# Last head of a fused retention and HGRN2 layer: its keys turned by VectorE and DMA, its level products 4 to 7 in pairs, and one output block's evacuations spread over four weight chunks

## The reference, cut to what matters

```python
h = rms_norm(x, norm_w) * (1 + scale) + shift
rq, rk, rv, rg, hq, hf_f, hf_b, hi, hg = split(h @ w_in, 9)
# retention, forward and on the flipped tokens
o_r = rms_norm(o_rf + flip(o_rb)) * silu(rg)
# HGRN2: f = lb + (1 - lb) * sigmoid(z), k = 1 - f, b = cumsum(log f) in a chunk
scores[i, j] = sum_d q[i, d] * k[j, d] * exp(b[i, d] - b[j, d])      # j <= i
o = scores @ v + (q * exp(b)) @ S
S = exp(b_last) * S + (k * exp(b_last - b)).T @ v
o_h = rms_norm(o_hf + flip(o_hb), hg_norm_w) * silu(hg)
y = rms_norm(x + gate * (concat(o_r, o_h) @ w_out), final_norm_w)
```

## Time and profile before

| | |
|---|---|
| median of 3 runs | 1402.6 us (1402.54 to 1402.9) |
| the profiled execution's own time | 1402.41 us |
| its span, first to last instruction | 1400.6 us |
| granted TensorE clock, mean | 0.999 of full speed |
| TensorE busy | 1383.0 us, 99% |
| VectorE / ScalarE / GpSimd busy | 1000.2 / 483.8 / 368.6 us |
| last head's scans among the first output block | about 1156 to 1227 us of the span |
| TensorE's last product ends | about 1392 us |

### The profile page before, as it was taken

The page is one execution under the profiler, slowest core; times in us unless marked ns, Lnnn a source line. Parts: engine busy times, 40 slices in busy tenths (PEclk is TensorE's granted clock), DMA queues, the critical chain, the costliest instruction groups (busy, mean ns, idle before and its releaser), DMA issues.

```text
span 1400.6 us, 24706 instructions
## 1 busy us (share of the span) xinstructions
PE 1383.0 (99%) x10042; PEld 1165.1 (83%) x10042; DVE 1000.2 (71%) x1330; ACT 483.8 (35%) x842; POOL 368.6 (26%) x292
## 2 busy tenths in 40 slices
PE   7999999999999999999999999999999999999997
PEld 5788898889888988898889888988898888888886
DVE  5555676667689888988888888877676768532345
ACT  4323243234333433342334333333333344221234
POOL 0000114311532153215321532153206225201220
PEclk9999999999999999999999999999999999999999
DMA  9994342434354535454444454433433358183235
GB/s 387 418 418 162 117 126 68 121 73 138 89 165 113 169 101 169 110 156 119 161 116 140 128 155 125 131 97 106 113 99 87 103 149 280 52 305 96 90 106 210
DMA packets 207735, 212.40 MB, mean 152 GB/s; under 512 B 144256, under 2 KB 156816, under 8 KB 202768
## 3 DMA queue, kind: packets, MB, share of 16 engines
q1 hardware_dynamic: 207600, 210.89, 48.0%
q10 hardware_dynamic: 32, 0.02, 0.0%
HBM read 182.27 MB, written 24.40 MB: 148 GB/s over the span
## 4 chain that ended last, share of the span: by engine, by line
PE 95%; DMA 3%; DVE 1%; SPq 0%; issue 0%; ACT 0%; DVEq 0%; ACTq 0%
PE ps L2133 10%; PE ps L2135 10%; PE ps L2134 10%; PE ps L1968 9%; PE ps L1969 8%; PE ps L1970 8%; PE ps L1944 8%; PE ps L2317 5%; PE ps L2319 5%; PE ps L2318 5%; DMA area<-in_w_mod 2%; PE ps L2150 2%; PE ps L1975 2%; PE ps L1976 2%; PE ps L1977 2%; PE ps L1934 2%
## 5 line engine op out<-in xcount | busy, mean ns | idle before, releaser
L1202 DVE TENSOR_TENSOR w_lo<-area,w_hi 128x1024 fp32r<-128x1024 f32 x143 | 190.4, 1331 | 206.3 <-ACT w_hi L730 206.3
L730 ACT ACTIVATE w_hi<-area 128x1024 fp32r<-128x1024 f32 x143 | 151.5, 1059 | 482.3 <-PE ps L2135 257.6
L2133 PE MATMUL ps<-w_hi,hT_hi 128*128 128x512 f32 x640 | 250.5, 391 | 0.0
L2135 PE MATMUL ps<-w_hi,hT_lo 128*128 128x512 f32 x640 | 249.1, 389 | 0.0
L2134 PE MATMUL ps<-w_lo,hT_hi 128*128 128x512 f32 x640 | 249.0, 389 | 0.0
L1968 PE MATMUL ps<-hT_hi,w_hi 128*128 128x512 f32 x512 | 204.8, 400 | 0.0
L1969 PE MATMUL ps<-hT_lo,w_hi 128*128 128x512 f32 x512 | 199.7, 390 | 0.0
L1970 PE MATMUL ps<-hT_hi,w_lo 128*128 128x512 f32 x512 | 199.6, 390 | 0.0
L2135 PEld LDWEIGHTS ps<-w_hi,hT_lo 128*128 128x128 f32 x640 | 120.1, 188 | 25.0
L2133 PEld LDWEIGHTS ps<-w_hi,hT_hi 128*128 128x128 f32 x640 | 120.2, 188 | 24.6
L2134 PEld LDWEIGHTS ps<-w_lo,hT_hi 128*128 128x128 f32 x640 | 120.2, 188 | 24.6
(11 more groups left out here) (282 smaller groups left out, 2426.5 us busy)
## 6 DMA issues: line engine op xcount, KB each, us to landing
area<-in_w_in SPq DMA_DIRECT2D x144, 512.0 KB, 4.3
area<-in_w_mod SPq DMA_DIRECT2D x26, 1024.0 KB, 12.3
area<-in_w_out SPq DMA_DIRECT2D x38, 512.0 KB, 3.8
gate_raw<-in_w_gate SPq DMA_DIRECT2D x32, 512.0 KB, 3.8
gate_raw<-in_w_mod SPq DMA_DIRECT2D x6, 1024.0 KB, 12.1
o_hi_scratch<-area SPq DMA_DIRECT2D x56, 80.0 KB, 2.4
o_lo_scratch<-area SPq DMA_DIRECT2D x56, 80.0 KB, 2.4
hT_hi<-o_hi_scratch SPq DMA_DIRECT2D x14, 320.0 KB, 7.2
```

What stands on the lines that cost most here:

```text
L730: act.activation(split_weights(h, n)[0], raw[:, n % 3, :], ACT.Copy).then_inc(wt_hi.sem, 1)
L1202: v.tensor_tensor(lo, raw[:, n % 3, :], hi.bitcast(F32), ALU.subtract).then_inc(wt_lo.sem, 1)
L2133: mm(out, hT_hi[:, k, tile_cols(t)], w_hi[:, n % 2, w], start=k == 0, stop=False)
L2135: i = mm(out, hT_lo[:, k, tile_cols(t)], w_hi[:, n % 2, w], start=False, stop=k == KT - 1)
```

## The change

1. **Keys.** `key_tokens` and `keys` go. The last head does as the others: `turn_keys(last)` at the end of VectorE's `items(17)`, so ahead of `own_decay(last, 0)`, and `move_keys(last)` in SyncE's queue between the third chunk of output weights and the stores of the retention states. TensorE's `chunk_updates` waits for the moved keys.
2. **Pairs.** TensorE issues product 4 and 5 one right after the other, a slice of the output block later than product 4 was, and product 6 and 7 likewise, where product 7 was. Products 5 and 7 get the PSUM bank C and the second quarter of DD, and `place` 4 to 7 wait for the second product of their pair. VectorE's order: `own_decay(5)` goes behind `differences(6)`, `place(6)` behind `own_decay(6)`, which leaves it ahead of `hgrn_silu(2)`.
3. **Evacuations.** In the last block, VectorE evacuates tiles 0 and 1 of the third block behind the second chunk as before, but then one tile behind each of chunks 2, 3 and 4 in place of three tiles behind chunk 2.

```diff
@@ PSUM of the scores
-                return ps[:, BB if product <= 2 else DD, 0:P]
+                return ps[:, BB if product <= 2 else DD, 0:P] if product not in (5, 7) else ps[:, DD, P:2 * P]
-            return C if following is not None and product in (5, 7) else A
+            return C if product in (5, 7) else A
@@ SyncE
             load_w_out(2)
+            move_keys(last)
             store_states(last, n_ret_f, n_ret_b, rst, r_state, r_state_stored)
             load_o(8)
             load_o(9)
@@ ScalarE
             decays(last, 2)
-            keys(last)
             split_w(2)
@@ VectorE, place
-                scored, placed = pe_level.at(h, (product if following is None else product | 1) + 1), h_sT.at(h, product)
+                scored = pe_level.at(h, (product if following is None and product < 4 else product | 1) + 1)
+                placed = h_sT.at(h, product)
@@ VectorE, items(17)
                     tokens_last(h)
-                    if not isinstance(h, int) or h < HEADS - 1:
-                        turn_keys(h)
+                    turn_keys(h)
@@ VectorE, last head
             split_w(4)
             place(last, None, 4)
             differences(last, 5)
-            own_decay(last, 5)
             place(last, None, 5)
             differences(last, 6)
-            place(last, None, 6)
+            own_decay(last, 5)
             split_w(5)
             own_decay(last, 6)
+            place(last, None, 6)
             hgrn_silu(last, 2)
             split_w(6)
             hgrn_silu(last, 3)
@@ VectorE, output blocks
+                    late = nb == OUT_BLOCKS - 1
                     if j == 1:
                         finish(nb - 1, 0, 2)
                     if j == 2:
-                        finish(nb - 1, 2, TILES)
+                        finish(nb - 1, 2, 3 if late else TILES)
+                    if late and j in (3, 4):
+                        finish(nb - 1, j, j + 1)
@@ TensorE, level_scores
-                    if following is None or product in (2, 4, 6):
+                    if product in (2, 4, 6) or following is None and product in (1, 3):
                         pe.wait_ge(h_sT.sem, h_sT.at(h, product))
@@ TensorE, last head
             first_block(1, 1, own)
-            pe.wait_ge(r_scaled.sem, r_scaled.at(last))
-            key_tokens(last)
             pe.wait_ge(h_sT.sem, h_sT.at(last, 3))
             for kk in range(WK):
                 first_block(0, kk, shared)
+            pe.wait_ge(r_scaled.sem, r_scaled.at(last))
             chunk_updates(last)
...
             first_block(3, 0)
+            first_block(3, 1)
             level_scores(last, None, 4)
-            first_block(3, 1)
             level_scores(last, None, 5)
             first_block(4, 0)
-            level_scores(last, None, 6)
             first_block(4, 1)
             first_block(5, 0)
+            level_scores(last, None, 6)
             level_scores(last, None, 7)
             first_block(5, 1)
             hgrn_outputs(last)
```

More of the change, by code:

```diff
@@ L325, in layer @@
         h_sq, h_rms, h_gated = Signal("h_sq"), Signal("h_rms", 2), Signal("h_gated")
-        last_keys, pe_hu, pe_level = Signal("last_keys", 2), Signal("pe_hu"), Signal("pe_level", PRODUCTS)
+        pe_hu, pe_level = Signal("pe_hu"), Signal("pe_level", PRODUCTS)
         pe_ho = Signal("pe_ho")
@@ L858, in retention_norm @@
                 i.then_inc(r_scaled.sem, 1)
[L860 to L864, removed]
             def context_states(h):
@@ L2201, in retention_columns, with chunk_updates @@
                 nc.tensor.transpose(ctx_columns(following), sT[:, 0:P], ident).then_inc(pe_columns.sem, 1)
-            def key_tokens(h):
-                pe.wait_ge(h_kl.sem, h_kl.at(h))
+            def chunk_updates(h):
+                pe.wait_ge(k_moved.sem, k_moved.at(h))
                 pe.wait_ge(r_S.sem, r_S.at(h))
                 pe.wait_ge(r_state.sem, r_state.at(h))
[L2208 to L2221, removed]
                 for i, t in enumerate((0, 1, 2, 3)):
```

## The result

| | before | after |
|---|---|---|
| median, 11 runs each | 1402.86 us (1402.33 to 1403.91) | 1406.49 us (1406.03 to 1408.81) |
| ratio, 95% interval | | 1.0028 (1.002 to 1.0036) |
| profiled execution: own time, span, granted clock | 1402.41, 1400.6, 0.999 | 1407.95, 1406.1, 0.997 |

Slower by 0.28%, 3.6 us of median, where 1406.5 was forecast.

The account below looks back on a forecast made before the run. TensorE's back-to-back row was taken as the bound. 1.5 - 0.87 + 0.3 - 0.4 + 1.7 + 2.35 - 0.6 = +4.0 us on 1402.41, median 1402.6, gave 1406.5; range 1403.7 to 1408.3.

Parts of the forecast that it names:

- retention outputs: First wait: TensorE waits 1.5 us for VectorE's retention chain, late behind key factors and turn; bounds 0.5 to 1.9.
- key transposes gone: TensorE's row before the slice's second product: without the 8 key transposes 0.87 us goes.
- third chunk: At `split_w(2)`, VectorE late with the low part: 0.3 us lost again, bounds 0.1 and 0.5.
- two pairs: Products 4 and 5, 6 and 7 paired: each pair saves 0.20, two save 0.4 us, to 0.6.
- product 7: Second wait: TensorE waits 1.7 us for GpSimd's last key product, part of it at `split_w(5)`; at most 2.5.
- HGRN2 outputs: Third wait: VectorE needs 6.4 us from product 7, TensorE arrives after 4.05; wait of 2.35 us, bounds 2.2 and 2.6.
- last block: With evacuations spread, TensorE's wait for a chunk's low part in the last block goes: 0.6 us saved, bounds 0 and 0.6.
- Rival (a): GpSimd and VectorE cross less: second wait goes, first shrinks to 0.5; +1.3, 1403.9, or +2.3, 1404.9; chance 0.22.
- Taking turns: VectorE and GpSimd instructions exclude each other; makes 1.0 of the first wait and all 1.7 of the second.
- (b): The queue is the bound: saved transfers come late, TensorE waits at `chunk_updates`; 1 to 2 us more, 1408; chance 0.12.
- (c): VectorE isn't late anywhere, its idle time covers the new order; the counted 1.9 us are gained, 1400.5; chance 0.04.
- (d): Spread evacuations don't free the chunk, GpSimd's weighting runs beside `split_w`: 0.6 more, 1407.1; inside the forecast's 0.62.

Follow-up runs that it names:

- experiment 3: Kernel before with only the spread evacuations of the last block: 1401.95 us, ratio 0.9993; a second time 1402.06, ratio 0.9996.
- experiment 7: Kernel before plus pairs and evacuations, no key change, VectorE's order from experiment 4, second pair and HGRN2 outputs one slice later on TensorE: 1402.58 us, ratio 0.9999.
- experiment 1: Kernel before with only the keys part: last head's keys turned by VectorE and DMA: 1403.73 us, ratio 1.0006.
- experiment 6: Changed kernel with GpSimd's key factors ahead of its first key product and ScalarE's key exponentials ahead of the first chunk's split: 1404.85 us, ratio 1.0018.
- experiment 9: Experiment 8 with `split_w(7)` ahead of the HGRN2 norm and gate and `split_w(2)` ahead of `differences(3)`: 1401.05 us, ratio 0.9988.
- experiment 4: Changed kernel with VectorE's last two `place` behind everything else, so `hgrn_silu(2)`, `split_w(6)` and `hgrn_silu(3)` come before them: 1406.46 us, ratio 1.0023.
- experiment 5: Changed kernel with `hgrn_silu(2)` ahead of `own_decay(6)`, then `place` 6 and 7, and only then `split_w(6)` and `hgrn_silu(3)`: 1403.9 us, ratio 1.0007.
- experiment 8: Changed kernel, all three parts, with the edits of experiments 4, 6 and 7 together: 1402.12 us, ratio 0.9996.
- experiment 2: Kernel before with only the pairs part (PSUM, `place`, VectorE's and TensorE's order), keys by TensorE: 1406.97 us, ratio 1.003.

## Why the prediction was right

The prediction had TensorE's row as what bounds the kernel, named the savings and the three waits with the engine behind each, and summed them to +4.0 us. All terms are there at about their sizes. "Measured" is the distance between neighbours on TensorE's row less what it would be unstopped.

| term | predicted | measured | where |
|---|---|---|---|
| retention outputs | +1.5 | +1.48 | 1166.39 against 1164.21 + 0.70, as before from 1163.93 to 1164.63 |
| key transposes gone | -0.87 | -0.95 | 1176.89 - 1170.29 = 6.60, before 1176.11 - 1168.56 = 7.55 |
| third chunk | +0.3 | +0.48 | 1180.78 - 1179.84, less two products of 0.23 |
| two pairs | -0.4 | -0.5 | TensorE is 1.26 us behind its old times at 1188.93 and 2.22 at 1209.48: 0.96, less the next row |
| product 7 | +1.7 | +1.45 | 1.12 of wait, 0.33 at `split_w(5)` |
| HGRN2 outputs | +2.35 | +2.25 | 6.30 less 4.05 |
| last block | -0.6 | -0.6 | no wait; 3 and 7 |
| granted clock | none | 0 to +1.7 | 1215.3 to 1219.8 |

Without the clock it sums to 1.48 - 0.95 + 0.48 - 0.5 + 1.45 + 2.25 - 0.6 = +3.6, and the median moved by 3.6. In the profiled execution, with 1.7 for the clock and 0.3 by which TensorE came later to the last head, it is 5.6; its last product began 1397.19 - 1391.60 = 5.6 later.

That 1406.5 was hit to the hundredth is luck. The forecast +4.0 was 0.4 too large, the largest part of it in product 7, and the kernel before ran at 1402.86 beside after, 0.26 above the 1402.6 that the forecast started from.

**The first wait** came as worked, through a chain of durations that each had a row. The end of the retention chain, 1166.13, was forecast at 1166.1, though TensorE in this execution stood 0.3 later than in that of before, so the chain was 0.3 us quicker than worked: the key factors took 2.96 in place of 2.83, but VectorE didn't wait 0.3 us ahead of its own product, which began at 1160.18 right behind the transposes. One reading on the way was loose: in the earlier trace rows the two instructions don't end together, VectorE's ends 0.35 us behind GpSimd's (1015.68 and 1015.33), as it would if it ran after it. Experiments 1 and 6 tie the wait to the key factors: moved ahead, it is gone, 1.6 us of median. The stop at the third chunk stays in experiment 6, so it doesn't hang on that wait.

**The pairs** save what was said, and a little more. 80 small products and the large one behind take 1196.50 - 1195.61 = 0.89 us to the next start and 0.34 to the one after, as in the earlier heads' 1.23. The prediction left open what stands ahead of a set: the last large product begins 0.32 us before it in place of 0.23 (before, 1206.45 and 1206.77), so a set that joins another saves 0.09 more. An undisturbed pair saves 0.3, two 0.6, the upper end of the 0.4 to 0.6 that was given. In after a wait stands inside the second pair and spoils part of it. Experiment 9 shows the sum from the other side: 0.95 + 0.6 + 0.6 less the stops of 0.33 and 0.23 is 1.6, and the distance is 1.65 us shorter.

**Product 7.** The chain from product 4's start, X = 1195.61, to the end of GpSimd's last key product took 13.3 us; 13.5 was forecast under the same load as before. TensorE wanted it at 1208.99 - 1.12 = 1207.87, X + 12.3 in place of X + 11.8; 0.3 of that it had lost at `split_w(5)` on the way, the rest is small steps that were left out of its row. The term was too large by the rest and by the 0.2 of the chain. Rival (a) needed the last key product to end before X + 11.8; it ended 1.5 us behind that.

**Taking turns** was called the weightiest assumption, and experiments 4 and 5 tested it on GpSimd's second half: 1.98 us with VectorE's `split_w(6)` beside it, 0.99 without, and the wait of TensorE 1.0 us longer. By the Trainium skill, SBUF — State Buffer, Who interferes with whom, a VectorE instruction with two SBUF inputs keeps out a GpSimd instruction that reads SBUF for its whole length, and the one that issues first has it. The trace agrees. It agrees too that a VectorE instruction with one SBUF input stays out of this: in after `place(4)`, which reads the scores from PSUM, and GpSimd's differences beside it (VectorE, then GpSimd) take 0.75 and 0.72 us.

```profile
1196.66 0.75 DVE L1501 COPY_PREDICATED area<-con,ps 128x512 f32<-128x512 int32 x1 [3.62 <-issue]
...
1196.32 0.72 POOL L1833 TENSOR_TENSOR area<-area 128x320 f32<-128x320 f32 x1 [5.09 <-PE ps L2147]
```

**The outputs' wait** rested only on the order of instructions, and experiments 4 and 5, which change only that, took it away entirely. I had expected the wait at product 7 to stay at 1.1 us in experiment 4. It grew to 2.1, since I had costed the new order by VectorE's row alone: the very rule of the first wait, two engines in turns, was left out.

**Rivals (b) to (d).** (b) The queue issued the write at 1160.29 and the four readers at 1165.97, and `chunk_updates` began at 1176.89 in its place behind a large product, without a wait; even in experiment 8, where the readers followed the write only after 9 us (1156.97, 1166.02), there was none. So the earlier turn bought nothing in the queue: the readers were issued at 1166.0 in both. The fourth chunk's load slipped to 1173.32, hidden as worked. (c) fell with the first wait. (d) The third block's chunk is free in time: no wait, and experiment 3 gave 0.7.

**Not foreseen: the clock.** The forecast had the sum right without it. The traced execution less its 1.7 us is 1406.25, close to the lowest of the 11 (1406.03), and the median agrees with the sum without the clock; so most executions of after seem to have run without the fall, though only this one was traced. What stays open is when it comes. Four executions of after lie within 0.2 us of its lowest, three 1.4 us or more above its median; with the same waits, 1.1 and 2.1 us, the profiled executions of experiments 2 and 6 keep the granted clock at 1.00 behind them. I have no experiment that sets it off at will.

## What to carry to other kernels

Where TensorE has no idle time, removing its work pays only as long as the engine that takes the work over isn't late: here 1.9 us of TensorE's work went, and three waits of 1.1 to 2.1 us came, each readable beforehand by adding up another engine's row up to TensorE's next need. When an instruction is moved on VectorE, look at which GpSimd instruction it will then stand beside, not only at VectorE's own row; and put whatever the next large products need (the low parts of weights) ahead of anything that waits for the scans. A pair of products is worth 0.2 to 0.3 us, a `place` behind the wrong instruction 2. And the view of waits doesn't list every stop: compare the distances between TensorE's starts as well.

## What the runs showed of the hardware

- TensorE's granted clock fell to the 1.2 GHz level in the middle of a kernel whose TensorE is busy 99% of the time, directly behind a wait of 2.1 us: in after with one of 1.1 us before it, over at 1208.99 (0.62 over 4.5 us, 1.7 us lost), in experiment 4 with none of over 0.3 us in the 40 us before it (0.50 over 3 us, about 1.5 us lost). In the profiled executions of experiments 2 and 6, with waits of 1.1 and 2.1 us in the same places, it stayed at 1.00.
- When VectorE and GpSimd both have instructions that exclude each other waiting (here tensor_tensor with all inputs in SBUF), they alternate. In experiment 4 the ends lie at 1207.00 (VectorE, 1206.17 + 0.83), 1207.88 (GpSimd), 1208.96 (VectorE), 1209.81 (GpSimd) and 1210.49 (VectorE): each comes behind the other's end by about its undisturbed length (0.87 us for GpSimd's, 1.15 for `split_w`, 0.8 for the last), so the stretch takes the sum of both rows, and neither engine is held for more than one instruction of the other. The same order of ends is in after from 1200.99 to 1204.21.
- A set of 40 products of 128x32 between large ones costs 0.7 us (before, 1207.60 - 1206.45 less two of 0.23), 80 in a row 1.1 (after, 1196.84 - 1195.29 less two of 0.23).
